# Rests of twelve weight quarters on GpSimd instead of VectorE, in the last two projections of the even layer

## What is computed

```python
xv, g_hy, q, k, v, g_att = _split(h @ w_in, EVEN_SPLITS)
x0, x1, v = _split(dw_conv(xv, conv_w, conv_b), (HY_WIDTH, HY_WIDTH, HY_WIDTH))
g = v * x1
hy = x0 * (bidir_long_conv(g, filt) + g * hy_bias)
y = concatenate([hy * silu(g_hy), att * silu(g_att)]) @ w_out
```

## Time and profile before

| | |
|---|---|
| time of three runs | 1782.91, 1783.67, 1783.99 us; median 1783.67 |
| span of the profiled execution (first to last instruction) | 1780.9 us; no time of its own is given beside it |
| instructions | 22805 |
| TensorE busy | 1732.2 us, 97% of the span |
| VectorE busy | 1164.9 us, 65% |
| ScalarE busy | 914.3 us, 51% |
| GpSimd busy | 49.4 us, 3% |
| mean granted TensorE clock | 0.996 of full speed |

### The profile page before, as it was taken

How to read it: one execution, slowest core, us unless ns; L and a number is a source line. 1 busy time by engine, 2 the same in 40 slices (tenths; PEclk the granted TensorE clock), 3 DMA queues, 4 the chain that set the end, 5 groups by cost and what they waited for, 6 DMA issues and landing times. The chain is left out here.

```text
span 1780.9 us, 22805 instructions
## 1 busy us (share of the span) xinstructions
PE 1732.2 (97%) x8527; PEld 1394.0 (78%) x8527; DVE 1164.9 (65%) x2141; ACT 914.3 (51%) x1490; POOL 49.4 (3%) x68
## 2 busy tenths in 40 slices
PE   8999999999998999999999999999999999999998
PEld 3776788777787877777777787788887787878886
DVE  6653466698437557767866775777646867577744
ACT  4333444333336356655656556467534756547743
POOL 0000000000000000000100002000000002000000
PEclk9999999999999999999999999999999999999999
DMA  9466211121425444443544444555554454555562
GB/s 333 155 200 226 95 56 64 54 70 67 142 95 175 132 125 146 147 139 107 180 147 153 147 154 155 176 177 193 198 189 157 127 175 134 183 165 183 189 218 76
DMA packets 115972, 267.23 MB, mean 150 GB/s; under 512 B 5412, under 2 KB 9837, under 8 KB 115672
## 3 DMA queue, kind: packets, MB, share of 16 engines
q1 hardware_dynamic: 111384, 252.26, 43.3%
q0 software_dynamic: 3504, 10.96, 2.0%
q10 hardware_dynamic: 976, 2.57, 0.4%
HBM read 264.63 MB, written 1.14 MB: 149 GB/s over the span
## 5 line engine op out<-in xcount | busy, mean ns | idle before, releaser
L146 DVE TENSOR_TENSOR qw_rest<-weights,qw_lead 128x1024 fp32r<-128x1024 f32 (+2 forms) x428 | 520.1, 1222 | 380.5 <-ACT qw_lead L334 375.3
L334 ACT ACTIVATE qw_lead<-weights 128x1024 fp32r<-128x1024 f32 (+2 forms) x428 | 446.4, 1048 | 461.5 <-PE psum L173 421.6
L173 PE MATMUL psum<-qw_lead,b_h_pair 128*128 128x512 f32 (+1 forms) x960 | 319.9, 398 | 3.3 <-ACT b_gates L2927 1.4
L173 PEld LDWEIGHTS psum<-qw_lead,b_h_pair 128*128 128x128 f32 x960 | 180.4, 188 | 43.8 <-issue 3.7
L173 PE MATMUL psum<-qw_rest,b_h_pair 128*128 128x512 f32 (+1 forms) x480 | 186.2, 388 | 0.0
L166 PE MATMUL psum<-b_h_pair,qw_lead 128*128 128x512 f32 x512 | 178.1, 392 | 2.0 <-DVE b_h_pair L713 2.0
L167 PE MATMUL psum<-b_h_pair,qw_rest 128*128 128x256 f32 x512 | 143.3, 280 | 0.0
L173 PE MATMUL psum<-e_h_lead,qw_lead 128*128 128x512 f32 x320 | 141.0, 441 | 1.8 <-DVE e_qT L1532 1.4
L173 PE MATMUL psum<-e_h_lead,qw_rest 128*128 128x512 f32 x320 | 125.7, 393 | 0.0
L173 PE MATMUL psum<-e_h_rest,qw_lead 128*128 128x512 f32 x320 | 124.9, 390 | 0.0
L166 PEld LDWEIGHTS psum<-b_h_pair,qw_lead 128*128 128x128 f32 x512 | 95.8, 187 | 23.7 <-DVE b_h_pair L713 2.9
(11 more groups left out here) (481 smaller groups left out, 3011.9 us busy)
## 6 DMA issues: line engine op xcount, KB each, us to landing
weights<-in_w_in SPq DMA_DIRECT2D x48, 1024.0 KB, 5.1
weights<-in_o_w_in SPq DMA_DIRECT2D x32, 1024.0 KB, 5.4
weights<-in_w_mlp_up SPq DMA_DIRECT2D x32, 1024.0 KB, 5.5
weights<-in_w_mlp_down SPq DMA_DIRECT2D x32, 1024.0 KB, 4.9
weights<-in_e_w_in SPq DMA_DIRECT2D x26, 1024.0 KB, 5.1
weights<-in_w_mod SPq DMA_DIRECT2D x24, 1024.0 KB, 7.1
weights<-in_e_w_out SPq DMA_DIRECT2D x8, 1024.0 KB, 4.9
weights<-in_o_w_out SPq DMA_DIRECT2D x8, 1024.0 KB, 4.9
```

What stands on the lines that cost most here:

```text
L146: return eng.tensor_tensor(self.rest[at], src, self.lead[at].bitcast(F32), ALU.subtract)
L173: mm = nc.tensor.matmul(out, l, r, start=start and i == 0, stop=stop and i == 2)
L334: self.core.nc.scalar.activation(self.buf.lead[self.at(u)], self.raw(u), ACT.Copy).then_inc(self.lead_ready, 1)
```

## The change

Of the 16 quarters 36 to 51, twelve get their rest from GpSimd: 37, 39, 41 and 43 of `e_x0`, and all of `e_ghy`, 44 to 51. The instruction is the same, on another engine, and it signals a semaphore of its own, since two engines can't count in order on one. PE waits for the one that made its quarter; SP waits for both where a half has a rest from each. To have a semaphore free, two of the long convolution are joined (`turned` and `tabs_turned`): the same instructions signal and wait as before, with the count shifted by one.

```diff
+        self.pool_rest_ready = keep("quarter_rest_by_pool")
+        lo, hi = self.split_no[self.first["e_x0"]], self.split_no[self.first["e_out"]]
+        self.by_pool = [i for i in range(lo, hi) if i >= lo + 8 or i % 2]
...
             dve.wait_ge(self.lead_ready, i + 1)
-            self.buf.take_rest(dve, self.at(u), self.raw(u)).then_inc(self.rest_ready, 1)
+            self.buf.take_rest(dve, self.at(u), self.raw(u)).then_inc(self.pool_rest_ready if i in self.by_pool else self.rest_ready, 1)
+    def rest_signal(self, i):
+        pooled = sum(m <= i for m in self.by_pool)
+        return (self.pool_rest_ready, pooled) if i in self.by_pool else (self.rest_ready, i + 1 - pooled)
     def parts(self, pe, u):
-        pe.wait_ge(self.rest_ready, self.split_no[u] + 1)
+        pe.wait_ge(*self.rest_signal(self.split_no[u]))
...
         for i, at in list(self.ahead())[:-1 if self.defer else None]:
-            yield at + self.offsets[1] + self.rests_later.get(i, 0.0)
-            self.core.stream.take_rest(dve, i)
+            if i not in self.core.stream.by_pool:
+                yield at + self.offsets[1] + self.rests_later.get(i, 0.0)
+                self.core.stream.take_rest(dve, i)
+    def pool_rests(self, pool):
+        for i, at in self.ahead():
+            if i in self.core.stream.by_pool:
+                yield at + self.offsets[1] - 0.2
+                self.core.stream.take_rest(pool, i)
...
             if h + w.RAW < len(w.halves):
                 sp.wait_ge(sem, value)
+                if h in also:
+                    sp.wait_ge(*also[h])
                 w.load(sp, h + w.RAW)
...
-        mm.then_inc(self.tabs_turned, 1)
+        mm.then_inc(self.tabs_then_turned, 1)
...
-            act.wait_ge(self.turned, n + 1)
+            act.wait_ge(self.tabs_then_turned, n + 2)
```

More of the change, by code:

```diff
@@ L402, in __init__ @@
         self.vector, self.scalar, self.sync = (self.rests,), (self.leads,), (self.loads,)
+        self.gpsimd = (self.pool_rests,)
     def ahead(self):
@@ L424, in rests @@
         for i, at in list(self.ahead())[:-1 if self.defer else None]:
-            yield at + self.offsets[1] + self.rests_later.get(i, 0.0)
-            self.core.stream.take_rest(dve, i)
+            if i not in self.core.stream.by_pool:
[6 more added lines that the diff above has]
+                self.core.stream.take_rest(pool, i)
     def loads(self, sp):
-        w, free = self.core.stream, []
+        w, free, also = self.core.stream, [], {}
         for i, at in ([(self.before.last_split(), -2.0)] if self.before else []) + list(self.ahead())[:-1 if self.defer else None]:
@@ L433, in loads @@
                 if w.last_of[w.units[u][0]] == u:
-                    free.append((w.units[u][0], at, w.rest_ready, i + 1))
+                    free.append((w.units[u][0], at, *w.rest_signal(i)))
+                    if i and (i - 1 in w.by_pool) != (i in w.by_pool) and w.units[w.split_units[i - 1]][0] == w.units[u][0]:
+                        also[w.units[u][0]] = w.rest_signal(i - 1)
         for m in self.raws:
@@ L1544, in __init__ @@
         s = lambda n: core.sem("lc_" + n)
-        self.turned, self.tok_ready, self.tabs_turned, self.tabs_ready = s("turned"), s("tok_ready"), s("tabs_turned"), s("tabs_ready")
+        self.tabs_then_turned, self.tok_ready, self.tabs_ready = s("tabs_then_turned"), s("tok_ready"), s("tabs_ready")
         self.spect, self.copied, self.read, self.made, self.folded = s("spect"), s("copied"), s("read"), s("made"), s("folded")
@@ L1565, in tables @@
             mm = self.core.nc.tensor.transpose(self.core.ps[:, self.banks[3], i * P:(i + 1) * P], self.room.tabs[:, i // 2, i % 2, :], self.core.ident[:])
-        mm.then_inc(self.tabs_turned, 1)
+        mm.then_inc(self.tabs_then_turned, 1)
     def tables_back(self, act):
         yield self.start - 2.8
-        act.wait_ge(self.tabs_turned, 1)
+        act.wait_ge(self.tabs_then_turned, 1)
         self.core.nc.scalar.activation(self.room.tabs[:, 2:4].rearrange("p e h n -> p (e h n)"), self.core.ps[:, self.banks[3], :], ACT.Copy,
@@ L1587, in turns @@
                 mm = nc.tensor.transpose(ps[:, self.banks[3], i * P:(i + 1) * P], self.gT[:, 4 * q + i, s * SEQ + t:(s + 1) * SEQ:2], self.core.ident[:])
-            mm.then_inc(self.turned, 1)
+            mm.then_inc(self.tabs_then_turned, 1)
     def tokens(self, act):
```

## The result

Four executions of the changed kernel took 1793.41 to 1796.36 us, median **1794.63**; four of the kernel before, beside them, 1782.91 to 1784.76, median 1783.83. The ratio is **1.0058**, 95% interval 1.0046 to 1.0070: slower by 10.8 us. The profiled execution has a span of 1791.6 (1780.9 before).

What follows compares the result with a forecast made beforehand. PE, busy 97%, bounds the kernel and hangs on VectorE at every round. PE idle of +9.2 us plus +5.1 of clock gives +14.3 on the 1780.9 span, 1795.2; with 2.8 around it 1798 us, range 1786 to 1802.

Steps and rivals of the forecast that it cites:

- The price of a rest on GpSimd: Moved rest beside VectorE's two-SBUF-input runs: 2.43 us from its start, holding VectorE 2.30; about 2.25 against 1.14 saved.
- D (2.58 for a hold): Rival: loss beyond the sum, hold 2.58 for 2.30 and half clock also behind idles of 1.8; 1803 us, chance 0.04.
- A (no turns): Rival: GpSimd and VectorE instructions do not hold each other, the rests are simply gone from VectorE; 1780.5, chance 0.08.
- Quarter 39: At the turns of the last `e_v` product: GpSimd's rest holds VectorE, PE's idle of 0.99 grows by 0.8 us.
- 41: Before the first inverse transform: GpSimd asks amid the products, delaying the folds and PE by 1.1 us.
- 45/46: Round two's products: both rests hold VectorE before the last fold, PE idle +3.2 us, without slack.
- 48/49: Round three's products: both rests hold VectorE, PE idle +2.9 us after a slack of 0.45.
- 51: Before the fourth inverse transform: falls beside instructions that read PSUM, PE's idle of 1.00 goes, -1.0 us.
- Quarter 43: Behind the first inverse: GpSimd asks before the rest of 42, delaying the taps; PE idle +2.2 us more.
- rival B: Turns, but VectorE is served first when it has instructions in line, GpSimd waits; 1780 to 1784 us, chance 0.08.
- Rival C: Turns, with the clock kept (1792.9) or the other order at quarter 43 (1789); chance 0.20.
- The clock: Behind three long new PE idles (3.7, 3.2, 2.9): half-clock stretches of 3.41 us, losing 1.7 each, +5.1 us.

Runs made afterwards that it cites:

- e7: Changed kernel with each of the twelve GpSimd rests made by two instructions of 512 columns: 1794.31 us, ratio 1.0060.
- e1: Against the kernel before, only the rests of quarters 37, 44, 47, 50 and 51 on GpSimd: 1781.73 us, ratio 0.9987.
- e6: Against the kernel before, only the rests of quarters 41 and 43 on GpSimd: 1783.83 us, one execution.
- e9: Against the kernel before, only rests 45 and 48 on GpSimd, asking amid round two's second and round three's third fold: 1786.22 us, one execution.
- e11: Against the kernel before, only rests 45 and 48 on GpSimd, asking amid round two's last product and round three's first fold: 1785.20 us, one execution.
- e5: Against the kernel before, only the rest of quarter 43 on GpSimd: 1785.31 us, one execution.
- e10: Against the kernel before, only rests 45 and 48 on GpSimd, each asking amid the last fold of its round: 1786.14 us, one execution.
- e2: Against the kernel before, only the rests of quarters 41, 45, 46, 48 and 49 on GpSimd: 1794.91 us, ratio 1.0058.
- e3: Changed kernel's same twelve rests on GpSimd, but GpSimd waits before them until the VectorE run is over: 1778.48 us, ratio 0.9963 to the kernel before.
- e8: Changed kernel again, no edit but a comment, for a second profile: 1796.66 us, span 1794.9.

## Why the prediction was right, and where it was not

The forecast was 1798 with a range of 1786 to 1802; 1794.63 lies in it, and the mechanism is in the main the one that it named: turns by whole instructions, which hold VectorE inside its dense runs and PE behind it. One term of the sum was wrong, and the clock's is right in size partly by luck. Step by step:

- **The price of a rest on GpSimd** (2.43 from its start, hold 2.30): 2.37 to 2.40 alone, and each held product 0.60 + 2.30 = 2.9. Right: the 2.43 is 0.03 to 0.06 too long. The other estimate that the prediction gives, 2.25, is 0.12 to 0.15 too short. With e7, turns by whole instructions stand, and rivals D (2.58 for a hold) and A (no turns) fall. That VectorE's busy time would not fall follows from it. GpSimd starts 0.07 to 0.08 after the lead (358.23 + 1.06 = 359.29, then 359.36), not 0.13 to 0.15.
- **Quarter 39, +0.8**: +0.74. **41, +1.1**: +1.21. **45/46, +3.2**: +3.1. **48/49, +2.9**: +2.9. **51, -1.0**: -1.1. **37, 44, 47, 50, 0**: 0, and e1 shows it by itself.
- **Quarter 43, +2.2: measured 0.** The step that failed is "the rest of 42, still VectorE's, asks at 360.74, behind GpSimd. It waits until 363.12". GpSimd did ask first, by 0.50 (the margin worked out was 0.32), and was still served second, in all four profiles where this meeting occurs (the changed kernel twice, e6, e7). The rule "who asks first is served first", taken from two meetings in the earlier trace rows, holds where VectorE is amid a product or a rest, and fails amid a fold (e9 to e11). This is rival B, at one kind of place only. Without this term the sum is 9.2 - 2.2 = 7.0, against 6.8 measured. Rival C had the other order at this place too, but its 1789 is worked out wrongly: it takes 2.2 and one stretch of clock (1.7) off 1792.9, a sum that has no clock in it. Taken off 1798 they give 1794.1, nearer to the measured 1794.63 than the forecast is. The Trainium skill, "SBUF — State Buffer", section "Who interferes with whom", says that a VectorE instruction with two SBUF inputs and a GpSimd one that reads SBUF exclude each other whole, and that the order of issue decides who waits. The first half agrees with every held row here; the second doesn't hold at the folds, where the measurement decides.
- **The clock, +5.1**: the term is about 1 too large (10.8 - 6.8 = 4.0 in the medians, 6.8 less 2.6 in the two profiles), and that it comes so near is partly luck. Three stretches were forecast and three came, but the one behind the 3.7 of quarter 43 could not come, since that idle never was; in its place stands one at the first inverse, behind 1.95. Two of the three lasted 6.83 and not 3.41, and 2.6 went off for stretches that happened to fall in the other execution. "The idle times of up to 1.45 are followed by none" was true of one execution: e5, e9, e10 and e11, with 0.75 and 1.45 there as before, each have a half-clock stretch of 3.41 at 361.66 to 362.72. And in the changed kernel an idle of 2.52 before 579.47 was followed by full clock, where the 2.49 of the earlier trace rows was not:

```profile
579.47 0.36 PE L173 MATMUL psum<-o_h_lead,qw_lead 128*128 128x256 f32 x1 [2.52 <-DVE ga L1552]
```

```profile
579.47:582.90 3.43, 2.39 (x16) 2.08 (x17) 2.46 (x10) 2.86 (x8) 0.00 (x0) 1.00 1.00 302
```

The idle times of 2.9 before the second inverse were followed by half clock in each of the four profiles that have them (the changed kernel twice, e2, e7); those of 2.7 before the third in three of four. At the first inverse all five profiles with the idle of 1.95 have a stretch, 6.83 long in four (the changed kernel twice, e2, e6) and 3.41 in e7; of the six with 0.75 (the kernel before, e1, e5, e9 to e11) four have one, of 3.41 each. So it comes without the longer idle too, and only a part of it can be put down to the change. A part of it cost nothing, because PE would have waited anyway: the idle before 362.66 is 0.77 instead of 1.45.
- **Edits at nothing** (SP's two waits, the joined semaphore, the MEMSET behind): behind quarter 36 every lasting step of the shift lies at a place of the table, so they cost nothing that shows.

Of the 3.5 by which the measured 10.8 falls short of 14.3, 2.2 lie at quarter 43 and about 1 in the clock. The cheaper reading, that VectorE had too much to do and GpSimd was free, is what e2 refutes and what e3 turns to use. Why a fold keeps GpSimd out and a product does not stays open: both are TENSOR_TENSOR of 128x512 float32 with both inputs in SBUF, 0.68 long, some of each without a semaphore wait ahead; nothing in the traces sets them apart, and no run changed the fold itself. All nine requests amid a fold came 0.10 to 0.17 into it; whether a later one would be served next was not tried.

## What to carry to other kernels

A second engine on the same kind of work isn't relief by itself: look in the trace for a place where both engines work with two SBUF inputs, read the price there, and lay the moved instruction beside instructions of the other engine that read PSUM or wait. If an engine's busy time stays as it was after work was taken off it, it is being held. A rule of who goes first that two meetings show is a rule for those two; where a term of a sum hangs on such a rule, work out the sum for the other order too, all its terms with it.

## What the hardware showed that I had not expected

- GpSimd's request amid one of VectorE's folds waits for the whole run behind it, up to four more instructions (5.70 from its start in place of 2.4); amid a product it waits for that product alone, as it did in all 22 such meetings (five in each of the changed kernel, e2, e7 and e8, one each in e6 and e11).
- One program's span differs by 3.3 us between two executions (1791.6 and 1794.9), and the granted clock of 0.50 comes in stretches of 3.41 or 6.83 us behind the same idle time or not at all. Matching the matmuls of two traces one by one separates this from the waits, which recur to 0.1 us; a difference of two spans does not.
